# The order of work at the entry to a layer's experts, in a two-block transformer kernel on one core

## The chip, the core and the metric

The kernel runs on one core of a Trainium2 chip. The core has a matrix engine (TensorE, PE in the rows, with its weight loads as PEld), a vector engine (VectorE, DVE), a scalar engine (ScalarE, ACT), a general engine (GpSimd, POOL) and a queue engine (SyncE, SP) that here issues nearly all transfers from device memory. On-chip memory has 128 partitions; matrix products land in eight banks called ps0 to ps7. The metric is the device time of one execution in microseconds (us), and lower is better.

## What is computed

Two blocks over 256 tokens of width 1024, all in 32-bit floats. The first block has two layers; each is a mixer followed by a mixture of experts, and only the latter matters here. Cut to its core:

```python
def moe_ffn(u, w_router, b_router, w1, w3, w2, ws1, ws3, ws2):
    scores = jax.nn.sigmoid(xf @ w_router)                 # 256 tokens x 64 experts
    biased = scores + b_router                             # 4 of 8 groups, then 8 of 64 experts
    ...
    w = w / (jnp.sum(w, axis=-1, keepdims=True) + 1e-20) * ROUTED_SCALE
    ...                                                    # each expert gets the list of its tokens
    out = (silu(x @ w1[e]) * (x @ w3[e])) @ w2[e]          # 64 experts, inner width 256
    shared = (silu(xf @ ws1) * (xf @ ws3)) @ ws2           # one more expert, for every token
    return routed + shared
```

The second block (a gated recurrence and windowed attention) follows and is not touched.

## The kernel before

Each engine has a program of its own, written as a Python generator; the order in the code is the order on that engine. Engines wait for each other by named events: `K.pe("x")` marks an event, `te.wait_ge(*(yield ("x",)))` waits for it.

**Experts.** A layer's 64 experts are handled in 25 passes of 1, 2 or 4 experts (`PASS`). In a pass, `pe_up` multiplies the selected tokens `x_b` by w1 and then by w3, ACT and DVE form silu(w1 part) times w3 part, `pe_turn` turns it, `pe_down` multiplies by w2, and `pe_scatter` adds the result to the sums in banks 0 to 3 while the next pass already runs. `pe_selected(a)` picks the token rows of the passes 2a and 2a+1 by products with one-hot matrices that DVE makes (`dve_select`); the rows h are held as a high and a low part (`hx_hi`, `hx_lo`, tile `exact_rows`) so that the picking is exact. Experts 0 to 5 are fixed; the others are ordered by the length of their lists, so that SP must read an expert's number (`by_rank`) before it can load its weights. That number is made by `pe_lists_turned`, `pe_lists_ranked` and `dve_ranked`.

**Weights.** Each expert has three matrices of 1 MB, 192 MB per layer. A ring of 11 places of 1 MB, four places in `ar` and one in `cst` hold them: 16 MB in all. SP issues the loads in one fixed order, the order of use (`in_turn`), and each load first waits until the former holder of its place is used up. One load that waits holds up all behind it. `places()` deals out the places: the one that comes free first, by a table of nominal times, takes the next load. In pass numbers (a pass p uses w1 until p+0.2, w3 until p+0.45, w2 until p+1), the entry's own weights have the times of `RING_HELD`: router -6, shared w1 and w3 together -4, shared down (ws2) -2. By this table the loads at the start of a layer wait as follows: w1 of expert 4 for the router, w1 of 5 and w3 of 4 for the shared w1 and w3, w3 of 5 for shared down, w2 of 4 and 5 for w1 of experts 0 and 1, w1 of 8 and 9 for w3 of 0 and 1, w3 of 8 and 9 for w2 of 0 and 1, w2 of 8 and 9 for w1 of 2 and 3 (pass 1), w1 of 32 and 33 for w3 of 2 and 3, w1 of 34 and 35 for w2 of 2 and 3, that is for the end of pass 1's down products.

**The entry** (`pe_moe_start`, `act_moe_start`, `dve_moe_start`). After the norm, PE computes the router's logits by experts (64 x 256, L1909), ACT copies them out, PE turns them to tokens (L1921), ACT takes the sigmoid. DVE then chooses the experts (L2022 to L2057, event `chosen`) while PE does the shared products with ws1 and ws3 and turns h (L1930). Next PE counts the places in the lists, does two of the four shared down products (L1947), the token lists of the passes 0 and 1, `pe_selected(0)`, the turn of the lists, the other two shared down products and the ranking of the lists. Then pass 0 begins. On DVE, the products silu x w3 part (L2074) and the four subtractions that make `hx_lo` (L2081) come ahead of the places in the lists (L2085). `hx_lo` is written over h itself, so these subtractions wait until PE has turned all of h.

Of the kernel before, what the change touches and what calls it, by code (L numbers as in the profile page):

```python
# [412 lines left out]
def ring_plan(K):  # L413
# [24 lines left out]
    def shared(l):  # L438

        K.plan(("up", l, EXPERTS), 2, [(lambda f: f[:, 0:UNIT], I["ws1"][l].rearrange("(p k) f -> p (k f)", k=8)),  # L440
                                       (lambda f: f[:, UNIT:2 * UNIT], I["ws3"][l].rearrange("(p k) f -> p (k f)", k=8))])
        K.plan(("down", l, EXPERTS), 1, [(lambda f: k_major(f, D, 2), I["ws2"][l].rearrange("(j p) n -> p j n", j=2))])
# [1458 lines left out]
def pe_moe_start(K, l):  # L1901
    te, h = K.te, K.h
    yield from pe_norm(K, ("ffn", l), 256, K.sq8)
    w = k_major(K.flat["router", l], EXPERTS)
    rb = yield from K.bank(("logits", l), only=7)
    te.wait_ge(*(yield ("ring", "router", l)))
    for kk in range(8):
        te.wait_ge(*(yield ("h", ("ffn", l), kk, 0)))
        ins = te.matmul(rb[0:64, 0:256], w[:, kk, :], h[:, kk, :], start=(kk == 0), stop=(kk == 7))  # L1909
    ins.then_inc(*K.pe("logits_ps", l, ps=rb))  # L1910
    K.pe.also("used", "router", l)
    w = K.flat["up", l, EXPERTS][:, 0:2 * UNIT].rearrange("p (m k f) -> p m k f", m=2, k=8)
    te.wait_ge(*(yield ("ring", "up", l, EXPERTS)))
    for j, bank in enumerate((4, 5)):
        b = yield from K.bank(("shared_g", l, j), only=bank)
        products(te, b[:, 0:256], [(w[:, 0, kk, j * P:(j + 1) * P], h[:, kk, :]) for kk in range(8)])
        if j == 0:
            rb = yield from K.bank(("scores", l), only=6)
            te.wait_ge(*(yield ("logits", l)))
            for i in range(2):  # L1920
                ins = te.transpose(rb[:, i * 64:(i + 1) * 64], K.t_b[0:64, i * P:(i + 1) * P], K.ident[0:64, 0:64])  # L1921
            ins.then_inc(*K.pe("logits_turned", l, ps=rb))
        products(te, b[:, 256:512], [(w[:, 1, kk, j * P:(j + 1) * P], h[:, kk, :])
                                     for kk in range(8)]).then_inc(*K.pe("shared_up", l, j, ps=b))
    K.pe.also("used", "up", l, EXPERTS)
    for i in range(2):
        for q in range(2):
            b = yield from K.bank(("hx_lo", l, i, q), only=(6, 4, 5, 3)[2 * i + q])
            for k in range(4):
                ins = te.transpose(b[:, k * P:(k + 1) * P], h[:, 4 * q + k, i * P:(i + 1) * P], K.ident)  # L1930
            ins.then_inc(*K.pe("h_turned", l, i, q, ps=b))
# [8 lines left out]
    w2 = k_major(K.flat["down", l, EXPERTS], D, 2)  # L1940
    te.wait_ge(*(yield ("ring", "down", l, EXPERTS)))
    te.wait_ge(*(yield ("shared_g", l, 1)))
    for n in range(4):
# [5 lines left out]
        if n == 1:
            yield from pe_first_slots(K, l)  # L1950
            yield from pe_selected(K, l, 0)
            yield from pe_lists_turned(K, l)
    ins.then_inc(*K.pe("shared_down", l))
    K.pe.also("used", "down", l, EXPERTS)
    yield from pe_lists_ranked(K, l)
# [37 lines left out]
def act_moe_start(K, l):  # L1993
# [4 lines left out]
    ac.activation(K.t_b[0:64, :], K.ps["logits_ps", l][0:64, 0:256], ACT.Copy).then_inc(*K.act("logits", l))  # L1998
    ac.wait_ge(*(yield ("logits_turned", l)))
    ac.activation(K.sc, K.ps["logits_turned", l][:, 0:128].rearrange("p (i e) -> p i e", i=2),  # L2000
                  ACT.Sigmoid).then_inc(*K.act("scores", l))
# [3 lines left out]
    for i in range(2):  # L2005
        for q in range(2):
            ac.wait_ge(*(yield ("h_turned", l, i, q)))
            ac.activation(K.hx_hi_r[:, i, q * 512:(q + 1) * 512], K.ps["h_turned", l, i, q][:, :],
                          ACT.Copy).then_inc(*K.act("hx_hi", l, i, q))


def dve_moe_start(K, l):
# [59 lines left out]
    for j in range(2):  # L2072
        ve.wait_ge(*(yield ("shared_silu", l, j)))
        ve.tensor_tensor(K.gs[:, j, :], K.ss[:, j, :], K.ps["shared_up", l, j][:, 256:512],  # L2074
                         ALU.mult).then_inc(*K.dve("shared_g", l, j))
    ve.wait_ge(*(yield ("h_turned", l, 1, 1)))
    for i in range(2):
        for q in range(2):
            cols = slice(q * 512, (q + 1) * 512)
            ve.wait_ge(*(yield ("hx_hi", l, i, q)))  # L2080
            ve.tensor_tensor(K.hx_lo_r[:, i, cols], K.ps["h_turned", l, i, q][:, :], K.hx_hi[:, i, cols],  # L2081
                             ALU.subtract).then_inc(*K.dve("hx_lo", l, i, q))
# [1906 lines left out]
```

## Time and profile before

| | |
|---|---|
| three timed runs | 2398.68, 2399.28, 2400.83 us; median 2399.28 |
| the profiled execution, its own time | 2398.06 us |
| span in its trace | 2396.8 us |
| PE busy in the span | 2309.0 us, 96% |
| DVE, ACT, POOL busy | 814.2, 570.1, 135.6 us |
| moved by DMA | 673.21 MB, mean 281 GB/s |
| stretch of the expert passes, layer 0 and layer 1 | about 407 to 908 us and 1288 to 1790 us |

Busy time of PE is the time in which some product was in flight, so 96% does not say that the products set the pace in every stage. A transfer's time counts from its issue on SP, and a stage can be short of data while the mean rate is low.

### The profile page before, as it was taken

To read this page: it belongs to the slowest core of one execution; us is meant where nothing else is said; L and a number is where in the kernel's file an instruction comes from. 1 tells how busy PE (TensorE), PEld (TensorE's weight loads), DVE (VectorE), ACT (ScalarE), POOL (GpSimd) and SP (SyncE) were. 2 spreads that over 40 slices of the span, in tenths; PEclk is the share of its full clock that TensorE was granted. 3 is DMA by queue.
4 is the path that set the end of the run, shared out by engine and by line. 5 is a ranking of instruction groups with operands and counts; after the bars stand their busy time and mean duration, and the time that the engine had idled before them with its cause. 6 is when DMAs were issued, how large, how long until landed. Compare 5 with 4: busy or idle time off the path is not lost.

```text
span 2396.8 us, 34579 instructions
## 1 busy us (share of the span) xinstructions
PE 2309.0 (96%) x14027; PEld 1650.0 (69%) x14027; DVE 814.2 (34%) x2133; ACT 570.1 (24%) x1231; POOL 135.6 (6%) x179
## 2 busy tenths in 40 slices
PE   7999999999998998999999999998989999999998
PEld 4868897676665665768887676666657777854764
DVE  0376623212121111486524122211223544421264
ACT  2234412111111112224211111111113343321264
POOL 4040000000000000100000000000000000000110
PEclk9999999999999999999999999999999999999999
DMA  9785684999999996855776999999993543141110
GB/s 336 273 294 190 228 338 188 408 418 417 417 418 418 418 418 256 309 180 191 285 300 242 407 418 420 418 418 417 418 375 121 182 156 110 71 150 53 71 71 18
DMA packets 194619, 673.21 MB, mean 281 GB/s; under 512 B 14000, under 2 KB 50072, under 8 KB 144528
## 3 DMA queue, kind: packets, MB, share of 16 engines
q1 hardware_dynamic: 187776, 656.87, 70.5%
q0 software_dynamic: 6240, 13.99, 1.7%
q8 instruction: 115, 1.88, 0.3%
q14 instruction: 56, 0.46, 0.1%
q10 hardware_dynamic: 432, 0.01, 0.0%
HBM read 661.38 MB, written 9.45 MB: 280 GB/s over the span
## 4 chain that ended last, share of the span: by engine, by line
PE 88%; DMA 7%; DVE 1%; ACT 1%; issue 1%; SPq 1%; DVEq 0%; ACTq 0%
PE ps L282 49%; PE ps L2175 13%; PE ps L2212 7%; DMA ring<-in_w 7%; PE ps L2228 4%; PE ps L1757 3%; PE ps L1207 1%; PE ps L695 1%; PE ps L2924 1%; PE ps L3537 1%; DMA ring<-in_w_in 1%; PE ps L3702 1%; PE ps L3685 1%; PE ps L2198 1%; PE ps L3694 1%
## 5 line engine op out<-in xcount | busy, mean ns | idle before, releaser
L282 PE MATMUL ps<-hT,ring 128*128 128x256 f32 (+2 forms) x2352 | 541.1, 386 | 3.2 <-ACT ar L1577 1.9
L282 PEld LDWEIGHTS ps<-hT,ring 128*128 128x128 f32 (+1 forms) x2352 | 438.5, 189 | 99.7 <-issue 37.1
L2175 PE MATMUL ps<-ring,ar 128*32 128x256 f32 (+2 forms) x2688 | 314.3, 389 | 8.6 <-DMA ar<-in_w 4.7
L2175 PEld LDWEIGHTS ps<-ring,ar 128*32 128x32 f32 (+2 forms) x2688 | 189.1, 126 | 96.8 <-issue 20.4
L2175 PE MATMUL ps<-ar 128*64 128x256 f32 (+2 forms) x1120 | 179.5, 388 | 9.1 <-DMA ring<-in_w 9.1
L2212 PE MATMUL ps<-ring,ar 128*64 128x512 f32 (+2 forms) x728 | 159.7, 612 | 12.6 <-DMA ring<-in_w 7.3
L2495 DVE TENSOR_TENSOR ar<-ar,ps 128x256 f32<-128x256 f32 x50 | 21.1, 422 | 437.0 <-PE ps L2175 437.0
L2519 DVE SCALAR_TENSOR_TENSOR exact_parts<-ps,ar,exact_parts 128x512 fp32r<-128x512 f32 x100 | 75.1, 751 | 215.0 <-ACT exact_parts L2363 209.4
L282 PE MATMUL ps<-ring,ar 128*128 128x512 f32 x320 | 140.3, 595 | 0.0
L2363 ACT ACTIVATE exact_parts<-ps,ar 128x512 fp32r<-128x512 f32 x100 | 68.7, 687 | 291.0 <-PE ps L2212 272.8
L2175 PEld LDWEIGHTS ps<-ar 128*64 128x64 f32 (+2 forms) x1120 | 102.7, 129 | 46.2 <-issue 11.8
L2228 PE MATMUL ps<-exact_parts 128*128 128x512 f32 x400 | 108.1, 409 | 3.4 <-DVE exact_parts L2519 3.4
L282 PEld LDWEIGHTS ps<-ring,ar 128*128 128x128 f32 x320 | 60.7, 191 | 72.1 <-issue 70.8
L282 PE MATMUL ps<-xT,ring 128*128 128x256 f32 x480 | 107.9, 381 | 1.0 <-DVE ar L2476 1.0
L282 PE MATMUL ps<-exact_parts,exact_rows 128*128 128x256 f32 x832 | 107.1, 282 | 0.0
L282 PEld LDWEIGHTS ps<-exact_parts,exact_rows 128*128 128x128 f32 x832 | 101.2, 189 | 4.0 <-issue 2.5
L282 PEld LDWEIGHTS ps<-xT,ring 128*128 128x128 f32 x480 | 90.2, 190 | 15.7 <-issue 2.5
L282 PE MATMUL ps<-ring,hT 128*128 128x256 f32 (+1 forms) x384 | 100.0, 417 | 0.0
L2228 PEld LDWEIGHTS ps<-exact_parts 128*128 128x128 f32 x400 | 70.9, 188 | 41.3 <-issue 14.9
L282 PE MATMUL ps<-ar,ring 128*128 128x256 f32 (+1 forms) x416 | 98.8, 396 | 0.0
L2212 PEld LDWEIGHTS ps<-ring,ar 128*64 128x64 f32 (+2 forms) x728 | 45.3, 127 | 74.3 <-issue 68.2
L1353 DVE SCALAR_TENSOR_TENSOR ar<-ar,wdw 128x256 f32<-128x256 f32 x240 | 95.8, 478 | 0.0
(461 smaller groups left out, 2813.8 us busy)
## 6 DMA issues: line engine op xcount, KB each, us to landing
ring<-in_w SPq DMA_DIRECT2D x259, 1024.0 KB, 21.1
ar<-in_w SPq DMA_DIRECT2D x100, 1024.0 KB, 18.5
ring<-in_w_mod SPq DMA_DIRECT2D x36, 2048.0 KB, 11.9
ring<-in_w_in SPq DMA_DIRECT2D x28, 2048.0 KB, 12.0
ring<-in_ab_w_in SPq DMA_DIRECT2D x46, 1024.0 KB, 11.3
cst<-in_w SPq DMA_DIRECT2D x25, 1024.0 KB, 18.0
ring<-in_w_out SPq DMA_DIRECT2D x4, 2048.0 KB, 10.1
ar<-in_ab_w_in SPq DMA_DIRECT2D x8, 1024.0 KB, 24.5
```

What stands on the lines that cost most here:

```text
L282: ins = te.matmul(o, l, r, start=(first and i == 0), stop=(last and i == len(pairs) - 1), skip_group_check=lax)
L695: ins = te.matmul(b[32 * t:32 * t + 32, :], col(2 * t + s), w[:, 2 * t + s, :], start=(s == 0), stop=(s == 1))
L1207: ins = te.matmul(b[:, :], h[:, kk, i * P:(i + 1) * P], w[0][:, kk, :], start=(kk == 0), stop=(kk == 7))
L1353: ins = ve.scalar_tensor_tensor(K.acc[:, c, :], K.hpad[:, c, k:k + 256], tap, K.acc[:, c, :], ALU.mult, ALU.add)
L1757: ins = te.matmul(b[:, 0:256], w[kk // 4][:, kk % 4, k::8], K.merged[:, kk, :], start=(kk == 0), stop=(kk == 7))
L2175: ins = te.matmul(b[cols, 0:256], K.x_b[:, kk, in_pair(p, cols)], w[r][:, kk, :], start=(kk == 0), stop=(kk == 7))
L2198: ins = te.transpose(b[:, j * P:(j + 1) * P], K.g_b[:, j::2], K.ident)
L2212: ins = te.matmul(b[cols, :], K.t_b[:, j * P + cols.start:j * P + cols.stop], weights_down(K, l, r, j, q), start=(j == 0), stop=(j == 1))
L2228: ins = te.matmul(K.banks[2 * i + q][:, :], K.wT_r[:, p % 2, i * P:(i + 1) * P], part[:, q * 512:(q + 1) * 512], start=False, stop=False, ...
L2363: ac.activation(K.o_hi_r[:, q * 512:(q + 1) * 512], K.ps["down", l, p, q][:, :], ACT.Copy, scale=K.slot[:, p, 1:2]).then_inc(*K.act("o_hi" ...
L2519: ve.scalar_tensor_tensor(K.o_lo_r[:, cols], K.ps["down", l, p, q][:, :], K.slot[:, p, 1:2], K.o_hi_r[:, cols].bitcast(F32), ALU.mult, ALU ...
L2924: ins = te.matmul(b[:, cols], w[:, kk, c * P:(c + 1) * P], h[:, kk, cols], start=(kk == 0), stop=(kk == 7))
```

## The change

The change reorders the entry, and the pieces that move are these.

- The router's product is done by tokens: the weights loaded into the array are 128 columns of h and the moving side is the 64 columns of the router, once per half of the tokens, into banks 7 and 6. The copy on ACT and the two turns of the logits are gone; the sigmoid reads the banks in two pieces.
- Shared w1 and shared w3 become two loads and two items of the ring with times of their own (-4 and -2); shared down gets the time 0.75.
- On PE both ws1 products come right behind the router, then the places in the lists, the ws3 product of the first half, the token lists of the passes 0 and 1, the turn of the lists, the ws3 product of the second half, the turns of h, `pe_selected(0)` and at once pass 0.
- The ranking of the lists stands inside pass 0, between its w1 and w3 products; the four shared down products stand between pass 0's turn and its down products.
- On DVE the places in the lists, the selection of passes 0 and 1 and the ranking come ahead of the shared products and of the subtractions, which move to a new function `dve_rows` and go by halves of the width (q) first.
- The loads' waits change with the table: w1 of 5 waits for ws1, w3 of 4 for ws3, w3 of 5 and w2 of 4 for w1 of 0 and 1, w2 of 5 and w1 of 8 for w3 of 0 and 1, w1 of 9 for shared down. The waits of w3 of 8 up to w1 of 35 stay as they were. Later, places swap among loads that are used in the same part of a pass, apart from one: the load of the first half of ("mod2", 0, 2), ahead of layer 1, waits for w2 of the last pass instead of w3 and w1.

```diff
-NOTHING, THIRD, OUT, ROUTER, SHARED_UP, SHARED_DOWN = -12, -10, -8, -6, -4, -2
+NOTHING, THIRD, OUT, ROUTER, SHARED_W1, SHARED_W3, SHARED_DOWN = -12, -10, -8, -6, -4, -2, 0.75
...
@@ pe_moe_start
-    rb = yield from K.bank(("logits", l), only=7)
+    rb = []
+    for i in range(2):
+        rb.append((yield from K.bank(("scores", l, i), only=7 - i)))
     te.wait_ge(*(yield ("ring", "router", l)))
     for kk in range(8):
         te.wait_ge(*(yield ("h", ("ffn", l), kk, 0)))
-        ins = te.matmul(rb[0:64, 0:256], w[:, kk, :], h[:, kk, :], start=(kk == 0), stop=(kk == 7))
-    ins.then_inc(*K.pe("logits_ps", l, ps=rb))
+        for i in range(2):
+            ins = te.matmul(rb[i][:, 0:64], h[:, kk, i * P:(i + 1) * P], w[:, kk, :], start=(kk == 0), stop=(kk == 7))
+    ins.then_inc(*K.pe("logits_ps", l))
...
+    for j in range(2):
+        b = K.ps["shared", l, j] = yield from K.bank(("shared_g", l, j), only=2 + j)
+        pairs = [(w[:, kk, j * P:(j + 1) * P], h[:, kk, :]) for kk in range(8)]
+        ins = products(te, b[:, 0:256], pairs)
+    ins.then_inc(*K.pe("used", "ws1", l))
...
+    pe_shared_w3(K, l, 0, range(8))
+    yield from pe_first_slots(K, l)
+    yield from pe_lists_turned(K, l)
+    pe_shared_w3(K, l, 1, range(8))
+    for q in range(2):
+        for i in range(2):
+            b = yield from K.bank(("hx_lo", l, i, q), only=(6, 0, 1, 5)[2 * q + i])
+            for k in range(4):
+                ins = te.transpose(b[:, k * P:(k + 1) * P], h[:, 4 * q + k, i * P:(i + 1) * P], K.ident)
+            ins.then_inc(*K.pe("h_turned", l, i, q, ps=b))
+    yield from pe_selected(K, l, 0)
...
@@ pe_up
+        if name == "w1" and p == 0:
+            yield from pe_lists_ranked(K, l)
@@ pe_experts
         yield from pe_turn(K, l, p)
+        if p == 0:
+            yield from pe_shared_down(K, l)
@@ act_experts
-        if p > 0:
-            ac.wait_ge(*(yield ("g", l, p - 1)))
+        ac.wait_ge(*(yield (("g", l, p - 1) if p > 0 else ("ranked_ps", l))))
@@ new, called from dve_experts after dve_slots
+def dve_rows(K, l):
+    ve = K.ve
+    for j in range(2):
+        ve.wait_ge(*(yield ("shared_silu", l, j)))
+        ve.tensor_tensor(K.gs[:, j, :], K.ss[:, j, :], K.ps["shared_up", l, j][:, 256:512],
+                         ALU.mult).then_inc(*K.dve("shared_g", l, j))
+    ve.wait_ge(*(yield ("h_turned", l, 1, 1)))
+    for q in range(2):
+        for i in range(2):
+            cols = slice(q * 512, (q + 1) * 512)
+            ve.wait_ge(*(yield ("hx_hi", l, i, q)))
+            ve.tensor_tensor(K.hx_lo_r[:, i, cols], K.ps["h_turned", l, i, q][:, :], K.hx_hi[:, i, cols],
+                             ALU.subtract).then_inc(*K.dve("hx_lo", l, i, q))
```

On PE, at the head of the entry (L1909 the router, L1921 the turns of the logits, L282 with `hT,ring` the shared products, L1930 the turns of h), before:

```order
L1909 MATMUL ps<-hT,ring 64x256 x8
L282 MATMUL ps<-hT,ring 128x256 x8
L1921 MATMUL ps<-cst,ar 128x64 x2
L282 MATMUL ps<-hT,ring 128x256 x24
L1930 MATMUL ps<-cst,hT 128x128 x16
```

and now (L1912 is the router; L282 with `ar` and `cst` are the places in the lists):

```order
L1912 MATMUL ps<-ring,hT 128x64 x16
L282 MATMUL ps<-hT,ring 128x256 x16
L282 MATMUL ps<-ar 128x64
L282 MATMUL ps<-ar,cst 128x64
L282 MATMUL ps<-ar 128x64
```

The eight wide router products became sixteen narrow ones, the turns of the logits are gone, and the places stand behind 16 of the 32 shared products and ahead of the turns of h.

On PE, from the places to pass 0 (L1947 shared down, L2138 the token lists, L282 with `exact_rows` is `pe_selected(0)`, L1973 and L1975 the turn of the lists, L1989 the end of the ranking), before:

```order
L1947 MATMUL ps<-ring,ar 128x512 x4
L2138 MATMUL ps<-ar,exact_parts 64x2 x8
L282 MATMUL ps<-exact_parts,exact_rows 128x256 x32
L1973 MATMUL ps<-cst,ar 64x128 x2
L1975 MATMUL ps<-cst,ar 64x128 x2
L1947 MATMUL ps<-ring,ar 128x512 x4
L282 MATMUL ps<-ar,cst 128x64
L282 MATMUL ps<-ar 128x64
...
L1989 MATMUL ps<-ar 128x64 x4
L2175 MATMUL ps<-cst,ar 64x256
```

and now (L2141 the token lists, L1985 and L1987 the turn of the lists, L1940 the turns of h, L2178 the first of pass 0's w1 products):

```order
L282 MATMUL ps<-hT,ring 128x256 x8
L2141 MATMUL ps<-ar,exact_parts 64x2 x8
L1985 MATMUL ps<-cst,ar 64x128 x2
L1987 MATMUL ps<-cst,ar 64x128 x2
L282 MATMUL ps<-hT,ring 128x256 x8
L1940 MATMUL ps<-cst,hT 128x128 x16
L282 MATMUL ps<-exact_parts,exact_rows 128x256 x32
L2178 MATMUL ps<-cst,ar 64x256
```

Nothing stands any more between the turns of h and `pe_selected(0)`, nor between that and pass 0; the ranking and the eight shared down products went into the pass.

On DVE (L2074 the shared products of silu, L2081 the subtractions, L2085 to L2089 the places in the lists, L2376 the selection of passes 0 and 1), before:

```order
L2071 COPY ar<-ar 128x128
L2074 TENSOR_TENSOR ar<-ar,ps 128x256 x2
L2081 TENSOR_TENSOR exact_rows<-ps,exact_rows 128x512 x4
L2085 SCALAR_TENSOR_TENSOR ar<-ps,ar 128x128
L2088 TENSOR_SCALAR ar<-ar 128x128
L2089 COPY ar<-ps 64x1
L2376 TENSOR_SCALAR exact_parts<-cst,ar 128x64 x8
```

and now (L2088 to L2092 the places, L2379 the selection, L2478 the shared products, L2485 the subtractions, L2495 the copies of the selected rows):

```order
L2085 COPY ar<-ar 128x128
L2088 SCALAR_TENSOR_TENSOR ar<-ps,ar 128x128
L2091 TENSOR_SCALAR ar<-ar 128x128
L2092 COPY ar<-ps 64x1
L2379 TENSOR_SCALAR exact_parts<-cst,ar 128x64 x8
...
L2386 COPY ar<-ps 128x2 x2
L2478 TENSOR_TENSOR ar<-ar,ps 128x256 x2
L2485 TENSOR_TENSOR exact_rows<-ps,exact_rows 128x512 x4
L2495 COPY ar<-ps 128x512 x2
```

The subtractions now come last, directly ahead of the copies of the selected rows.

## Rows read from the trace of the kernel before

**Rows 1.** The page's chain that ended last, shares by engine.

```profile
PE 88%; DMA 7%; DVE 1%; ACT 1%; issue 1%; SPq 1%; DVEq 0%; ACTq 0%
```

**Rows 2.** That chain at the ends of both expert stretches: start, us, what.

```profile
875.85 26.64 DMA ring<-in_w
...
1754.08 30.33 DMA ring<-in_w
```

**Rows 3.** Stretches of the experts: length, busy by engine, clock, DMA share, GB/s.

```profile
437.00:438.00 1.00, 1.00 (x14) 0.64 (x12) 0.58 (x1) 0.38 (x1) 0.00 (x0) 1.00 1.11 295
438.00:439.00 1.00, 1.00 (x12) 0.70 (x10) 0.17 (x1) 0.00 (x0) 0.00 (x0) 1.00 0.50 164
438.60:902.50 463.90, 439.03 (x3580) 297.69 (x3576) 94.33 (x283) 59.97 (x102) 7.57 (x14) 0.99 1.02 417
...
1318.00:1320.00 2.00, 2.00 (x22) 1.34 (x20) 0.75 (x1) 0.02 (x1) 0.00 (x0) 1.00 0.91 270
...
1319.00:1784.50 465.50, 440.76 (x3583) 298.95 (x3578) 94.43 (x283) 59.97 (x102) 7.57 (x14) 0.99 1.01 415
```

**Rows 4.** SP's issues of loads in order of time: start, us, what.

```profile
411.30 0.33 SPq L579 DMA_DIRECT2D cst<-in_w  x1
...
436.84 1.44 SPq L579 DMA_DIRECT2D ring<-in_w  x2
```

**Rows 5.** PE in order of time, layer 0's entry: start, us, what, idle before.

```profile
370.92 5.32 PE L1909 MATMUL ps<-hT,ring 128*64 128x256 f32 x16 [2.23 <-ACT hT L1110]
376.18 3.72 PE L282 MATMUL ps<-hT,ring 128*128 128x256 f32 x16
379.83 0.34 PE L1921 MATMUL ps<-cst,ar 64*128 64x64 f32 x2
...
390.56 2.19 PE L1930 MATMUL ps<-cst,hT 128*128 128x128 f32 x16
392.58 0.33 PE L282 MATMUL ps<-ar 128*128 128x64 f32 x2
392.75 0.39 PE L282 MATMUL ps<-ar,cst 128*128 128x64 f32 x2
392.97 0.39 PE L282 MATMUL ps<-ar 128*128 128x64 f32 x2
...
394.06 3.70 PE L1947 MATMUL ps<-ring,ar 128*128 128x512 f32 x8
...
398.27 3.90 PE L282 MATMUL ps<-exact_parts,exact_rows 128*128 128x256 f32 x32
402.01 0.38 PE L1973 MATMUL ps<-cst,ar 128*64 128x128 f32 x2
...
407.57 0.43 PE L2175 MATMUL ps<-cst,ar 128*64 128x256 f32 x1
...
416.44 3.66 PE L2212 MATMUL ps<-ar 128*64 128x512 f32 x16 [0.61 <-DVE ar L2383]
419.90 7.11 PE L2175 MATMUL ps<-ring,ar 128*64 128x256 f32 x64
```

**Rows 6.** DVE in order of time, same place.

```profile
380.58 0.29 DVE L2022 TENSOR_TENSOR ar<-ar,par 128x128 f32<-128x128 f32 x1 [7.37 <-ACT ar L2000]
...
385.72 0.29 DVE L2057 TENSOR_TENSOR ar<-ar 128x128 f32<-128x128 f32 x1
...
392.78 2.48 DVE L2081 TENSOR_TENSOR exact_rows<-ps,exact_rows 128x512 fp32r<-128x512 f32 x4 [1.19 <-PE ps L1930]
...
402.21 0.69 DVE L2476 COPY ar<-ps 128x512 f32<-128x512 f32 x1 [1.12 <-PE ps L282]
```

**Rows 7.** Stretches of the router in layer 0 and layer 1, columns as in group 3.

```profile
370.94:374.35 3.41, 3.41 (x8) 1.82 (x9) 2.27 (x7) 2.63 (x7) 0.00 (x0) 0.50 1.01 428
...
1251.58:1254.99 3.41, 3.41 (x9) 1.81 (x10) 2.27 (x7) 2.62 (x7) 0.00 (x0) 0.50 1.01 428
```

**Rows 8.** Weight loads of 128 columns early in the run, half clock, then full: busy us, mean ns.

```profile
L1207 PEld LDWEIGHTS ps<-ring,hT 128*128 128x128 f32 x2 | 0.7, 337 | 1.0 <-ACT hT L1110 0.5 <-issue 0.5
...
L1207 PEld LDWEIGHTS ps<-ring,hT 128*128 128x128 f32 x21 | 4.0, 190 | 5.0 <-issue 5.0
```

More of the change, by code:

```diff
@@ L438, in shared @@
     def shared(l):
[L440 to L441 removed]
+        for n in ("ws1", "ws3"):
+            K.plan((n, l), 1, [(lambda f: f, I[n][l].rearrange("(p k) f -> p (k f)", k=8))])
         K.plan(("down", l, EXPERTS), 1, [(lambda f: k_major(f, D, 2), I["ws2"][l].rearrange("(j p) n -> p j n", j=2))])
@@ L1908, in pe_moe_start @@
         te.wait_ge(*(yield ("h", ("ffn", l), kk, 0)))
-        ins = te.matmul(rb[0:64, 0:256], w[:, kk, :], h[:, kk, :], start=(kk == 0), stop=(kk == 7))
-    ins.then_inc(*K.pe("logits_ps", l, ps=rb))
+        for i in range(2):
+            ins = te.matmul(rb[i][:, 0:64], h[:, kk, i * P:(i + 1) * P], w[:, kk, :], start=(kk == 0), stop=(kk == 7))
+    ins.then_inc(*K.pe("logits_ps", l))
     K.pe.also("used", "router", l)
[L1912 to L1925, printed above, removed]
-    for i in range(2):
[L1927 to L1931, printed above, removed]
+    for i in range(2):
+        K.ps["logits_ps", l, i] = rb[i]
+    w = k_major(K.flat["ws1", l], 256)
+    te.wait_ge(*(yield ("ring", "ws1", l)))
+    for j in range(2):
[3 more added lines that the diff above has]
+    ins.then_inc(*K.pe("used", "ws1", l))
+    te.wait_ge(*(yield ("ring", "ws3", l)))
     b = yield from K.bank(("places", l), ("counted", l), only=7)
@@ L1939, in pe_moe_start, with pe_shared_w3, pe_shared_down @@
                                     for i in range(2)]).then_inc(*K.pe("ranks", l, ps=b))
-    w2 = k_major(K.flat["down", l, EXPERTS], D, 2)
+    pe_shared_w3(K, l, 0, range(8))
[9 more added lines that the diff above has]
+    yield from pe_selected(K, l, 0)
+def pe_shared_w3(K, l, j, of):
+    w, b = k_major(K.flat["ws3", l], 256), K.ps["shared", l, j]
+    ins = products(K.te, b[:, 256:512], [(w[:, kk, j * P:(j + 1) * P], K.h[:, kk, :]) for kk in of],
+                   first=(0 in of), last=(7 in of))
+    if 7 in of:
+        ins.then_inc(*K.pe("shared_up", l, j, ps=b))
+    if j == 1:
+        K.pe.also("used", "ws3", l)
+def pe_shared_down(K, l):
+    te, w2 = K.te, k_major(K.flat["down", l, EXPERTS], D, 2)
     te.wait_ge(*(yield ("ring", "down", l, EXPERTS)))
@@ L1948, in pe_moe_start @@
                             stop=False, skip_group_check=True)
[L1949 to L1955, printed above, removed]
+    ins.then_inc(*K.pe("used", "down", l, EXPERTS))
 def pe_first_slots(K, l):
@@ L1997, in act_moe_start @@
     ac.wait_ge(*(yield ("logits_ps", l)))
[L1998 to L2001, printed above, removed]
+    for i in range(2):
+        ac.activation(K.sc[:, i, :], K.ps["logits_ps", l, i][:, 0:64], ACT.Sigmoid).then_inc(*K.act("scores", l, i))
     for j in range(2):
@@ L2004, in act_moe_start @@
         ac.activation(K.ss[:, j, :], K.ps["shared_up", l, j][:, 0:256], ACT.Silu).then_inc(*K.act("shared_silu", l, j))
-    for i in range(2):
-        for q in range(2):
+        if j == 0:
+            ac.wait_ge(*(yield ("lists_ps", l)))
+            ac.activation(K.turned_lists[0:64], K.ps["lists_ps", l][0:64, :].rearrange("p (a n) -> p a n", a=4),
+                          ACT.Copy).then_inc(*K.act("lists_turned", l))
+    for q in range(2):
+        for i in range(2):
             ac.wait_ge(*(yield ("h_turned", l, i, q)))
@@ L2071, in dve_moe_start @@
     ve.tensor_copy(K.tok_w[:, :, :, 1], mk).then_inc(*K.dve())
[L2072 to L2082, printed above, removed]
     ve.wait_ge(*(yield ("ranks", l)))
@@ L2484, in dve_experts @@
             yield from dve_slots(K, l, p)
+        yield from dve_rows(K, l)
         yield from selected(0)
```

11 lines of the change are left out of this document (5 added, 6 removed).

## The prediction

> **What bounds the kernel now.** The chain that ended last was read first. Its shares [rows 1] give PE 88% and DMA 7%, which reads like a kernel held by its products. The chain's pieces in order of time tell more: both expert stretches end on a transfer [rows 2]. The last weights of layer 0 were issued at 875.85 and landed 26.64 us later, at 902.49; in layer 1 it was 30.33 us from 1754.08. So the second view was the stretches [rows 3], and there the reader should compare the DMA share with PE's busy time. From 438.6 to 902.5, 463.9 us, the transfers ran at a share of 1.02 and 417 GB/s without a break, while PE was busy for 439.03 us: 24.9 us of it was spare. Layer 1 reads the same (465.5 us, 1.01, PE 440.76). The transfers set the end of both stretches, and PE waits for them on the way.
>
> A stream that never stops ends a fixed time after it last started. Where it last started is the question for this change. The single microseconds before that show it [rows 3]: 295 GB/s from 437 to 438 and 164 from 438 to 439. SP had issued the next two loads only at 436.84 [rows 4]; these are w1 of 34 and 35, which wait for the w2 places of pass 1. Layer 1 shows the like: 270 GB/s from 1318 to 1320 [rows 3]. All 16 MB were full or in use, and nothing was left to fetch until PE ended pass 1. So **the end of an expert stretch follows the time at which PE ends pass 1's down products**, us for us, and what the entry does earlier counts only as far as it moves that. The third view was therefore PE and DVE in order of time through the entry [rows 5, 6].
>
> PE has almost no hole there. From the router's first product at 370.92 to the end of pass 0's down products, at 419.90 where the next products start [rows 5], its only wait is the 0.61 us ahead of L2212, for a copy on DVE.
>
> **The change, part by part.** R is the time at which the router ends, 376.18 before.
>
> *Router.* Eight products of 256 columns become sixteen of 64; every 32-bit product shows as two rows, so 32 rows. At full clock two rows with 128 loaded columns and 64 moving ones take 0.22 us, from 392.75 to 392.97 [rows 5], so 0.11 each. In both layers the granted clock is at half, 1.2 GHz, for 3.41 us from the router's first product on, behind PE's wait of 2.23 us [rows 5, 7]. A weight load of 128 columns takes 337 ns at half and 190 ns at full clock [rows 8], so I take twice the pace, 0.22. Then 3.41 us hold 15.5 rows, the other 16.5 take 1.8 us, and R is 376.1: -0.1 us. The bounds: all 32 at 0.11 end at 374.4 (-1.8), all at 0.22 at 377.9 (+1.7).
>
> The Trainium skill, page "TensorE: Matmul & The Clock Gate", section "LDWEIGHTS (loading the stationary operand)", says that a weight load costs by its columns, P/1.2 ns, whatever the depth: 107 ns for 128 columns, which the trace's 0.11 us bears out at full clock. Its formula makes no difference between the clocks; by it alone the router would take 32 x 0.107 = 3.4 us and a layer would gain 1.8 us here. The two durations of the weight load differ with the clock, and I go by them.
>
> *Turns of the logits.* L1921 goes, with 0.3 us of PE [rows 5]. The copy on ACT goes too; neither it nor the sigmoid was on PE's path.
>
> *Choice and places.* Before, DVE began 0.41 us behind the end of L1921 at 380.17, which is one sigmoid with its hand-overs, and was done with `chosen` at 386.01, 5.43 us later [rows 5, 6]. Two sigmoid pieces cost at most twice that, so `chosen` comes by R+6.3. PE meanwhile does the ws1 products: 16 rows took 3.65 us [rows 5], so 32 take 7.3. The places don't wait; the margin is 1.0 us, and beyond it every us counts in full. The rest of DVE's list work then lies beside the ws3 products, two times 3.65 us, and is at no cost. The places, token lists, turn of the lists and ranking are the same products as before, in another place: nothing.
>
> *Subtractions.* Here a stall arises. Behind the turns of h PE now has `pe_selected(0)`, whose first half needs the first two pieces of `hx_lo`, and DVE starts these only when all of h is turned. Before, the turns ended at 392.58, DVE began at 392.78 and took 2.48 us for four [rows 5, 6]; PE had places, shared down and token lists to do until 398.27. Now it waits 0.2 + 2 x 0.6 = 1.4 us. The second half needs the other two 1.2 us later, while PE is busy for 1.87 us (half of 398.27 to 402.01), so that costs nothing. Bounds: 0.8, if one piece were in time, and 2.7, if PE waited for all four.
>
> *Copies of the selected rows.* w1 of pass 0 waits for all of `x_b`. The last copy on DVE began at 402.21, 0.2 us behind the products' end at 402.01, and took 0.69 [rows 5, 6]. Before, 5.5 us of other products lay over it; now nothing does: with the hand-over 0.95 us (0.7 to 1.1).
>
> *Ranking and shared down inside pass 0.* The ranking delays ACT's silu, but w3's products follow it on PE, so that is hidden. Shared down now stands where PE waited for the turned g, and its length covers the 0.61 us [rows 5]: -0.6.
>
> *Loads.* Shared down, two blocks of about 3.7 us, and the short ranking went into pass 0, and 0.6 us left it [rows 5]. With an end 1.35 us later it begins about 7 us earlier than 407.57, and w1's places come free 7 us earlier than 411.30 [rows 4]. But those transfers are the ones that filled the time up to 437 before; the next pair still waits for the end of pass 1. The load for w1 of 9 now waits for shared down, near 418; pass 3 uses it tens of us later. The swapped places later on are used up in the same parts of a pass. The one exception, a 2 MB load ahead of layer 1, goes out some 10 us later and needs about 5 us; the norm and the first projection of layer 1 stand before its use.
>
> Sum for one layer: 1.4 + 0.95 - 0.6 - 0.3 - 0.1 = **+1.35 us** at the end of pass 0, hence of pass 1 and of the stretch. Two layers: +2.7 us. The profiled execution took 2398.06 us, of which the span is 2396.8; with the change 2400.8. The median of the runs shown is 1.2 us above it, so they should give **2402.0 us**.
>
> **The rivals.**
>
> *The clock stays down (slower).* The new router loads weights for as long as it moves columns; the old one kept the array streaming. In the rows every rise to 2.4 GHz came after a stretch of dense products, and no row shows work like the new router's at half clock. If it does not lift the clock, all its rows run at half, R is 377.9, and the ws1 products run at half for as long as the old router did, 3.41 us [rows 7], before the clock rises: 1.8 + 1.7 = 3.5 us more in a layer. Then 2402.0 + 2 x 3.5 = **2409.0**. For it: that difference. Against it: PE is never idle in the new router, and another execution may not fall to half here at all, since 2.23 us is a short wait. It decides from the point where the clock is still at half 3.41 us after the first router product.
>
> The same page of the Trainium skill, section "Part 4: PE-mode transpose", says that transposes do not bring the full clock since they don't count as busy in the same way. No run here shows that; if the like holds for products bound by weight loads, this rival is what happens.
>
> *The earlier transfers win (faster).* Places come free up to 7 us earlier. If the stream did not run dry again before w1 of 34, each layer would gain up to those 7 us: 2399.3 - 14 = **2385**. For it: the long idle of the transfers ahead of 411 goes. Against it: ten loads of 1 MB lie between 411.3 and 437 and take 25 us at 417 GB/s, they end just as the pair at 436.84 is issued, and the last of them wait for w3 of pass 1, which does not come earlier. It decides by the GB/s around the end of pass 1.
>
> *The two stalls are longer.* All four subtractions on the path and 1.1 us for the copies: +2.8 a layer, **2404.9**.
>
> **How the numbers follow.** A measurement here can tell about 0.2%, 4.8 us, from no change. I give the forecast 0.57, with a range of its own from 2398.5 (the router at its lower bound) to 2404; the clock 0.30; the longer stalls 0.05; the earlier transfers 0.08. Forecast: same. Clock and longer stalls: slower, 0.35. Earlier transfers: faster, 0.08. For 8 in 10 the range runs from 2398.5 to the clock's case with half a us to spare, 2409.5.
>
> **What would show it.** In the new profile: waits of PE of about 1.4 us ahead of `pe_selected(0)`, for the subtractions, and of 0.95 us ahead of pass 0's w1, for the copies; no wait ahead of pass 0's down products; transfers that run dry again where pass 1 ends, at a time some 1.3 us later than 436.84; then no break to the end of the stretch. The clock rival shows as a granted clock of half beyond 374.4. The prediction is wrong if PE ends pass 1 earlier than before, if the transfers do not stop there, or if the stretch from there to the last landing is not the same length as before.

## The result and the profile after

The changed kernel takes 2406.4 us (median of 11 runs, 2402.95 to 2411.24) against 2399.0 (11 runs): a ratio of 1.0034, 95% interval 1.0026 to 1.0041. That is 6.2 to 9.8 us more, slower by a third of a per cent. The time lies inside the forecast range, but not with the case that was held likeliest (2402.0); it lies nearer to the rival in which the clock stays down (2409.0). The interval, 2405.2 to 2408.8 us, holds neither.

The profiled execution took 2410.87 us with a span of 2409.6. It is among the longest of the eleven, so its 12.8 us over the span of before is more than the median difference; where they lie is counted below.

The page's chain that ended last, shares by engine, of the changed kernel:

```profile
PE 87%; DMA 8%; DVE 2%; ACT 1%; issue 1%; SPq 1%; POOL 0%; DVEq 0%; ACTq 0%
```

and that chain in order of time (start, us, what), at the ends of both expert stretches:

```profile
879.23 27.45 DMA ar<-in_w
...
1764.63 31.00 DMA ring<-in_w
```

The shares say nothing new: the kernel is bound as before, and both stretches still end on a landing. The landings are what to read: 906.68 and 1795.63 us, against 902.49 and 1784.41 in [rows 2], so 4.2 and 11.2 us later.

The stretches of the changed kernel (length, busy by engine, granted clock, DMA share, GB/s), first both routers, then the ends of pass 1 and what follows them:

```profile
370.09:380.33 10.24, 10.15 (x40) 9.55 (x41) 4.84 (x28) 5.65 (x11) 0.00 (x0) 0.50 0.78 306
1257.56:1267.80 10.24, 10.24 (x39) 9.34 (x39) 5.27 (x32) 4.91 (x10) 0.00 (x0) 0.50 0.82 316
440.00:441.00 1.00, 1.00 (x10) 0.56 (x8) 0.72 (x2) 0.37 (x1) 0.00 (x0) 1.00 0.49 197
441.00:442.00 1.00, 1.00 (x14) 0.65 (x10) 0.65 (x1) 0.32 (x1) 0.00 (x0) 1.00 0.66 115
442.00:443.00 1.00, 1.00 (x12) 0.64 (x10) 0.10 (x1) 0.00 (x0) 0.00 (x0) 1.00 0.57 164
442.60:906.70 464.10, 439.37 (x3580) 298.80 (x3576) 94.34 (x283) 59.96 (x102) 7.57 (x14) 0.99 1.02 417
1328.00:1330.00 2.00, 2.00 (x22) 1.30 (x20) 0.75 (x1) 0.12 (x1) 0.00 (x0) 1.00 0.74 164
1329.50:1795.63 466.13, 442.75 (x3580) 299.14 (x3576) 94.43 (x283) 59.96 (x102) 7.57 (x14) 0.99 1.01 415
```

Two things stand here. The granted clock is at half for 10.24 us from the router on, in both layers, where [rows 7] had 3.41 us. And the transfers run dry at the end of pass 1 as before, about 4 us later than in [rows 3], and then run at 417 GB/s for 464.1 us: the stretch kept its length (463.9) and was only moved.

SP's first load for pass 0 in the changed kernel (start, us, what), 4 us earlier than in [rows 4]:

```profile
407.30 0.33 SPq L579 DMA_DIRECT2D cst<-in_w  x1
```

PE in order of time through layer 0's entry of the changed kernel (start, us, what, idle before):

```profile
370.18 7.06 PE L1912 MATMUL ps<-ring,hT 128*128 128x64 f32 x32 [2.23 <-ACT hT L1110]
377.04 8.75 PE L282 MATMUL ps<-hT,ring 128*128 128x256 f32 x32
385.63 0.33 PE L282 MATMUL ps<-ar 128*128 128x64 f32 x2
...
395.26 1.91 PE L1940 MATMUL ps<-cst,hT 128*128 128x128 f32 x16
398.64 4.00 PE L282 MATMUL ps<-exact_parts,exact_rows 128*128 128x256 f32 x32 [1.47 <-DVE exact_rows L2485]
403.59 0.40 PE L2178 MATMUL ps<-cst,ar 128*64 128x256 f32 x1 [0.94 <-issue]
...
413.08 0.50 PE L2203 MATMUL ps<-cst,ar 128*128 128x128 f32 x2
413.42 7.03 PE L1965 MATMUL ps<-ring,ar 128*128 128x512 f32 x16
420.38 3.66 PE L2217 MATMUL ps<-ar 128*64 128x512 f32 x16
423.87 0.38 PE L2178 MATMUL ps<-ring,ar 128*64 128x256 f32 x2
```

and at the head of layer 1's entry:

```profile
1256.91 6.47 PE L1912 MATMUL ps<-ring,hT 128*128 128x64 f32 x32 [2.23 <-ACT hT L1110]
1263.18 2.45 PE L282 MATMUL ps<-hT,ring 128*128 128x256 f32 x5
```

From the router's first product to the first product behind pass 0's down products is the measure for all that follows; call it the entry. It was 48.97 us, from 370.92 to 419.90 [rows 5], and is 53.69 now. The difference of 4.7 us can be read off line by line. The router takes 6.86 us to the next start, 1.6 more than 5.26. The 32 rows of ws1 take 8.59 where the same rows take 7.0 at full clock (in a run below), so 1.6 more. The two new idle times are 1.47 and 0.94. The 0.61 us ahead of the down products is gone, and so are 0.3 us for the turns of the logits. That makes 4.7.

DVE in order of time, the instruction that ends the choice (`chosen`) and then the two new idle times:

```profile
382.86 0.29 DVE L2071 TENSOR_TENSOR ar<-ar 128x128 f32<-128x128 f32 x1
...
397.21 2.48 DVE L2485 TENSOR_TENSOR exact_rows<-ps,exact_rows 128x512 fp32r<-128x512 f32 x4 [0.91 <-PE ps L1940]
...
402.69 0.69 DVE L2495 COPY ar<-ps 128x512 f32<-128x512 f32 x1 [1.19 <-PE ps L282]
```

The subtractions begin when all of h is turned, and PE starts 1.43 us behind their start, after two of the four. The last copy ends at 403.38, and w1's products begin 0.2 us later: the idle time that the view puts down to "issue" ends on a copy of DVE.

The 12.8 us of the profiled execution: -0.7 up to the first router, +4.7 and +4.8 for the entries (53.75 us in layer 1), +0.2 and +1.1 for what follows an entry up to the last landing, +1.2 between the landing of layer 0 and the router of layer 1, +1.6 behind the last landing. The small ones are no part of the change that could be named: in each of the ten traces the clock also falls at other places, and the median difference is smaller. The swapped load ahead of layer 1 shows no price: from the landing of layer 0 to the router of layer 1 the six kernels built on the changed one took 345.7 to 350.5 us, the four built on the kernel before 347.0 to 350.0.

### The profile page after: what moved, and what is told of

Same layout as the page of the kernel before. It is cut to its first block, busy times and chain, and to the rows that moved or that the text cites. A ratio compares the mean times of both kernels' runs of the same rounds, so it can differ in the third digit from the quotient of the medians.

```text
span 2409.6 us, 34633 instructions
## 1 busy us (share of the span) xinstructions
PE 2319.0 (96%) x14055; PEld 1660.2 (69%) x14055; DVE 814.4 (34%) x2133; ACT 569.2 (24%) x1231; POOL 135.7 (6%) x179
## 4 chain that ended last, share of the span: by engine, by line
PE 87%; DMA 8%; DVE 2%; ACT 1%; issue 1%; SPq 1%; POOL 0%; DVEq 0%; ACTq 0%
PE ps L282 49%; PE ps L2178 13%; PE ps L2217 7%; DMA ring<-in_w 6%; PE ps L2233 3%; PE ps L1757 3%; PE ps L1207 1%; PE ps L695 1%; PE ps L2944 1%; PE ps L3557 1%; DMA ar<-in_w 1%; DMA ring<-in_w_in 1%; PE ps L3705 1%; PE ps L2203 1%; SPq L579 1%
## 5 line engine op out<-in xcount | busy, mean ns | idle before, releaser
L282 PE MATMUL ps<-hT,ring 128*128 128x256 f32 (+2 forms) x2352 | 546.9, 388 | 3.2 <-ACT ar L1577 1.9
L282 PEld LDWEIGHTS ps<-hT,ring 128*128 128x128 f32 (+1 forms) x2352 | 442.5, 191 | 100.3 <-issue 36.4
L2178 PE MATMUL ps<-ring,ar 128*64 128x256 f32 (+2 forms) x2704 | 336.0, 390 | 10.6 <-DMA ar<-in_w 6.3
L2178 PEld LDWEIGHTS ps<-ring,ar 128*64 128x64 f32 (+2 forms) x2704 | 200.8, 127 | 99.6 <-issue 22.4
L2178 PE MATMUL ps<-ar 128*64 128x256 f32 (+2 forms) x1072 | 206.5, 389 | 7.1 <-DMA ring<-in_w 7.1
L2217 PE MATMUL ps<-ring,ar 128*32 128x512 f32 (+1 forms) x704 | 170.2, 616 | 13.5 <-DVE ar L2386 6.1
L2178 PEld LDWEIGHTS ps<-ar 128*64 128x64 f32 (+2 forms) x1072 | 113.9, 129 | 46.7 <-issue 15.7
L282 PE MATMUL ps<-ring,ar 128*128 128x512 f32 x320 | 139.8, 593 | 0.9 <-DVE ar L3786 0.9
L282 PE MATMUL ps<-exact_parts,exact_rows 128*128 128x256 f32 x832 | 107.8, 283 | 2.9 <-DVE exact_rows L2485 2.9
L282 PEld LDWEIGHTS ps<-ring,ar 128*128 128x128 f32 x320 | 60.3, 190 | 72.8 <-issue 70.7
L282 PE MATMUL ps<-xT,ring 128*128 128x256 f32 x480 | 108.7, 381 | 1.0 <-DVE ar L2495 1.0
L282 PEld LDWEIGHTS ps<-exact_parts,exact_rows 128*128 128x128 f32 x832 | 101.9, 189 | 7.3 <-DVE exact_rows L2485 3.4
L2217 PE MATMUL ps<-ar 128*32 128x512 f32 (+2 forms) x280 | 104.4, 632 | 1.2 <-DVE ar L2386 1.2
L282 PEld LDWEIGHTS ps<-xT,ring 128*128 128x128 f32 x480 | 90.4, 190 | 15.3 <-issue 2.1
L282 PE MATMUL ps<-ring,hT 128*128 128x256 f32 (+1 forms) x384 | 100.0, 417 | 0.0
L282 PE MATMUL ps<-ar,ring 128*128 128x256 f32 (+1 forms) x416 | 98.8, 396 | 0.0
L2217 PEld LDWEIGHTS ps<-ring,ar 128*32 128x32 f32 (+1 forms) x704 | 47.8, 127 | 70.7 <-issue 67.1
## 6 DMA issues: line engine op xcount, KB each, us to landing
ring<-in_ab_w_in SPq DMA_DIRECT2D x46, 1024.0 KB, 11.2
```

The source lines that it names most:

```text
L282: ins = te.matmul(o, l, r, start=(first and i == 0), stop=(last and i == len(pairs) - 1), skip_group_check=lax)
L2178: ins = te.matmul(b[cols, 0:256], K.x_b[:, kk, in_pair(p, cols)], w[r][:, kk, :], start=(kk == 0), stop=(kk == 7))
L2217: ins = te.matmul(b[cols, :], K.t_b[:, j * P + cols.start:j * P + cols.stop], weights_down(K, l, r, j, q), start=(j == 0), stop=(j == 1))
```

## The experiments

All ratios are to the kernel before, run on the same chip (2398.1 us for the new router alone, the old router, the clock held in the changed kernel and the waits covered; 2398.31 for the other four).

**The new router alone.** The kernel before with the new router's products, its two sigmoids, and no turn of the logits:

```diff
-        ins = te.matmul(rb[0:64, 0:256], w[:, kk, :], h[:, kk, :], start=(kk == 0), stop=(kk == 7))
+        for i in range(2):
+            ins = te.matmul(rb[i][:, 0:64], h[:, kk, i * P:(i + 1) * P], w[:, kk, :], start=(kk == 0), stop=(kk == 7))
...
-            te.wait_ge(*(yield ("logits", l)))
-            for i in range(2):
-                ins = te.transpose(rb[:, i * 64:(i + 1) * 64], K.t_b[0:64, i * P:(i + 1) * P], K.ident[0:64, 0:64])
```

> The kernel before with the new router alone: 32 rows of 64 columns, no copy and no turn of the logits. Theory (the clock stays down through such a router): the granted clock is at half for about 10 us from the router's first product instead of 3.41; router +1.6 us, shared products behind it +1.5, turns -0.3, so +2.8 us in a layer and 2404.6 us, about two thirds of the whole slowdown. Rival (the slowdown is the two new stalls and the moved loads; the router itself costs nothing): the turns alone are gone, 2398.4 us, at half clock for 3.41 us as before.

Measured: 2402.95 us, ratio 1.0023 (1.0014 to 1.0033), which is 3.4 to 7.9 us more. The router alone makes the kernel slower. Its profiled execution shows both cases, since the clock fell in layer 1 and not in layer 0 (stretches of that kernel, columns as above):

```profile
366.98:370.58 3.60, 3.60 (x33) 3.60 (x33) 2.29 (x7) 3.58 (x8) 0.00 (x0) 1.00 1.03 435
1247.30:1257.54 10.24, 10.24 (x40) 9.43 (x40) 5.12 (x31) 5.11 (x10) 0.00 (x0) 0.50 0.84 323
```

In layer 0 the same 32 rows took 3.60 us at full clock and the entry 46.82 us; in layer 1 the clock was at half for 10.24 us and the entry took 51.77. One program, one execution, and 4.95 us between its two layers.

**The old router in the changed kernel.** Its logits are copied and turned at once:

```diff
-        for i in range(2):
-            ins = te.matmul(rb[i][:, 0:64], h[:, kk, i * P:(i + 1) * P], w[:, kk, :], start=(kk == 0), stop=(kk == 7))
+        ins = te.matmul(rb[0:64, 0:256], w[:, kk, :], h[:, kk, :], start=(kk == 0), stop=(kk == 7))
...
+    rb = yield from K.bank(("scores", l), only=6)
+    te.wait_ge(*(yield ("logits", l)))
+    for i in range(2):
+        ins = te.transpose(rb[:, i * 64:(i + 1) * 64], K.t_b[0:64, i * P:(i + 1) * P], K.ident[0:64, 0:64])
```

> The changed kernel with the old router, eight products of 256 columns, whose logits are copied and turned at once behind it. Theory (clock): half clock for 3.41 us only, which takes 3.1 us off a layer, while PE waits about 0.7 us for the copy and turns for 0.3, so -2.1 a layer and 2402.2 us. Rival (the stalls and the moved loads): nothing is taken off and the turn adds 1.0 a layer, 2408.4 us.

Measured: 2404.53 us, ratio 1.0024 (1.0014 to 1.0035), 3.4 to 8.4 us more than before. By the time alone this doesn't decide: it lies between the two expectations, and its interval overlaps that of the changed kernel. The trace does (a stretch, then PE in order of time):

```profile
370.74:374.16 3.42, 3.42 (x9) 1.82 (x10) 2.23 (x7) 2.60 (x7) 0.00 (x0) 0.50 1.01 426
374.16:377.57 3.41, 2.94 (x15) 1.87 (x14) 0.00 (x0) 1.50 (x2) 0.00 (x0) 1.00 0.99 332
```

```profile
370.69 5.32 PE L1909 MATMUL ps<-hT,ring 128*64 128x256 f32 x16 [2.23 <-ACT hT L1110]
376.48 0.33 PE L1915 MATMUL ps<-cst,ar 64*128 64x64 f32 x2 [0.47 <-ACT ar L2010]
376.74 1.56 PE L282 MATMUL ps<-hT,ring 128*128 128x256 f32 x6
```

With the old router the clock is back after 3.4 us, and the entries take 51.18 and 51.25 us: 2.5 less than the changed kernel, 2.2 more than before.

**The clock held through the wait.** Four products on constants, read by nothing, in PE's idle time ahead of the router; the same in the changed kernel and in the kernel before:

```diff
+    pe_keep_busy(K, rb[0], 4)
     te.wait_ge(*(yield ("ring", "router", l)))
```

In the changed kernel:

> The changed kernel with four products of 256 columns on constants, whose result nothing reads, in PE's wait of some 2.3 us ahead of the router. Theory (clock): it does not fall there, the router's 32 rows take 3.5 us in place of 7.06 and ws1's products 7.1 in place of 8.59, so -4.9 us a layer and 2396.6 us; the places don't wait, since the choice ends 6.1 us behind the router and ws1 takes 7.1. Rival (the clock is no part of the slowdown, or the end of the stretch doesn't follow PE): 2406.4 us.

In the kernel before:

> The kernel before with the same four products on constants in PE's wait ahead of its router. Theory (what the clock costs is read from the router): the old router loses only the one stretch of 3.41 us at half clock, so its layer gains 1.6 us and the whole 3.2: 2394.9 us against 2398.1 for the kernel before in the last runs. The changed kernel gained 8.2 us from the same products. Rival (the products bring something else than the clock, the same for both kernels): 2390 us.

Measured: 2398.16 us in the changed kernel, ratio 1.0000 (0.9991 to 1.0009), and 2396.66 in the kernel before, ratio 0.9995 (0.9986 to 1.0004). The same four products take the changed kernel from 1.0034 to no difference, and do little for the kernel before. Both gained less than expected, 8.2 of 9.8 us and 1.2 to 1.7 of 3.2; a likely reason stands under the table. PE in order of time, the changed kernel with them:

```profile
367.49 1.89 PE L681 MATMUL ps<-cst 128*128 128x256 f32 x8
369.89 3.76 PE L1913 MATMUL ps<-ring,hT 128*128 128x64 f32 x32 [0.51 <-ACT hT L1110]
373.48 7.13 PE L282 MATMUL ps<-hT,ring 128*128 128x256 f32 x32
380.44 0.33 PE L282 MATMUL ps<-ar 128*128 128x64 f32 x2
```

and the kernel before with them:

```profile
368.30 3.64 PE L1910 MATMUL ps<-hT,ring 128*64 128x256 f32 x16 [0.51 <-ACT hT L1110]
371.86 3.72 PE L282 MATMUL ps<-hT,ring 128*128 128x256 f32 x16
```

The stretch behind the router's start in each, first the changed kernel:

```profile
369.89:380.13 10.24, 10.24 (x63) 9.46 (x64) 7.65 (x43) 5.55 (x11) 0.00 (x0) 1.00 0.85 341
368.30:371.71 3.41, 3.41 (x16) 2.06 (x16) 2.28 (x7) 2.64 (x7) 0.00 (x0) 1.00 1.03 435
```

With the clock at full the two routers take the same time, 3.59 and 3.56 us. The entries are 48.66 and 48.71 us in the changed kernel, 47.42 and 47.43 in the kernel before: 1.25 us apart.

**The two waits covered.** Shared down is split over them:

```diff
+    yield from pe_shared_down(K, l, (2, 3))
     yield from pe_selected(K, l, 0)
+    yield from pe_shared_down(K, l, (0,))
...
         if p == 0:
-            yield from pe_shared_down(K, l)
+            yield from pe_shared_down(K, l, (1,))
```

> The changed kernel with shared down split: its third and fourth quarter stand behind the turns of h, over the subtractions, its first behind the products that select pass 0's rows, over the copies, its second stays in pass 0. Theory (the end of a stretch follows PE's entry us for us): the stalls of 1.47 and 0.94 us go, -2.4 us a layer, 2401.6 us; the clock's part, some 6 us, stays. Rival (the transfers set the end whatever PE's entry does): no change, 2406.4 us.

Measured: 2402.43 us, ratio 1.0016 (1.0007 to 1.0025). Against the changed kernel's 1.0034 that is 4 us less, near the 4.8 expected. PE in order of time shows both idle times gone:

```profile
395.45 3.60 PE L1967 MATMUL ps<-ring,ar 128*128 128x512 f32 x8
398.48 4.22 PE L282 MATMUL ps<-exact_parts,exact_rows 128*128 128x256 f32 x32
402.54 1.88 PE L1967 MATMUL ps<-ring,ar 128*128 128x512 f32 x4
```

Its entries are 50.92 and 51.04 us, 2.7 less, and the clock is still at half for 10.24 us in both layers.

**Wide moving columns.** The changed kernel's router, order and weight loads as they are, but each row moves its 64 columns four times (the copies are read by nothing):

```diff
-            ins = te.matmul(rb[i][:, 0:64], h[:, kk, i * P:(i + 1) * P], w[:, kk, :], start=(kk == 0), stop=(kk == 7))
+            ins = te.matmul(rb[i][:, 0:256].rearrange("p (a e) -> p a e", a=4), h[:, kk, i * P:(i + 1) * P],
+                            w[:, kk, :].unsqueeze(1).to_broadcast([P, 4, 64]), start=(kk == 0), stop=(kk == 7))
```

> The changed kernel whose router moves each 64 weight columns four times: the same 32 rows and the same weight loads of 128 columns, but 256 moving columns a row as in the old router. One look, for the clock. Theory (it is the narrow moving side that does not lift the clock): where the clock falls to half at the router, it is back at full 3.41 us later, as with the old router; the 32 rows take about 3.41 + 24 x 0.22 = 8.7 us, the ws1 products behind them 7.1. Rival (it is the weight loads, or the order by tokens): half for 10.24 us, the 32 rows at some 0.43 each.

Measured: one run, 2403.75 us, of which the trace is what counts. In layer 0 the clock did not fall. In layer 1 it did (stretches, then PE in order of time):

```profile
1250.39:1253.81 3.42, 3.42 (x9) 2.68 (x9) 1.40 (x5) 3.04 (x6) 0.00 (x0) 0.50 1.00 419
1253.81:1257.22 3.41, 3.41 (x17) 2.98 (x16) 0.00 (x0) 0.00 (x0) 0.00 (x0) 1.00 0.47 192
```

```profile
1249.49 8.83 PE L1912 MATMUL ps<-ring,hT 128*128 128x256 f32 x32 [2.23 <-ACT hT L1110]
1258.16 7.07 PE L282 MATMUL ps<-hT,ring 128*128 128x256 f32 x32
```

The clock was back after 3.4 us, in the middle of the router, where the narrow rows were at half for 10.24 us in all five of their falls. The order by tokens and the loads of 128 columns are the same in both, so neither of them explains the longer stretch; what differs is the moving side. This rests on one fall in one execution. The rows took 8.67 us to the next start, as expected.

**Delay put in by hand.** Sixteen products on constants ahead of the ranking, in the kernel before:

```diff
     b = yield from K.bank(("ranked_kept", l))
+    pe_keep_busy(K, b, 16)
```

> The kernel before with sixteen more products of 256 columns on constants ahead of the ranking, before pass 0: some 6.9 us of PE's time a layer that changes nothing else. Theory (the end of an expert stretch follows PE's entry us for us): pass 1 ends 6.9 us later and so does the last landing, +13.8 us, 2411.9 us. Rival (the transfers set the end, PE has slack): 2398 to 2401 us.

Measured: 2411.86 us, ratio 1.0057 (1.0044 to 1.0071), 13.5 us over the median of before: us for us. Layer 1's entry, where the clock fell as before, took 55.89, which is 6.92 more. The added products in layer 0, and the landings that end both stretches:

```profile
403.76 7.07 PE L681 MATMUL ps<-cst 128*128 128x256 f32 x32
```

```profile
880.08 26.86 DMA ring<-in_w
...
1765.17 31.09 DMA ring<-in_w
```

The landings stand at 906.94 and 1796.26 us, 482.3 and 484.3 behind the entries' ends, as before (482.6 and 483.9).

**Both remedies.** The changed kernel with the four products and the split:

> The changed kernel with the four products ahead of the router and the split shared down together. From the router's first product to the end of pass 0's down products it should take 48.66 - 2.77 = 45.9 us a layer, against 48.98 in the kernel before. Theory (us for us in this direction too): -3.1 us a layer, 2391.9 us, faster than both kernels. Rival (below the length of before, the transfers that fill the time up to the end of pass 1 become the bound): 2396 to 2398 us.

Measured: 2394.68 us, ratio 0.9987 (0.9977 to 0.9996): faster than both kernels, by 1.0 to 5.5 us against the one before. Its entries are 45.97 and 46.02 us as expected, but the time stands between the 2391.9 expected and the rival's 2396. Some of that is the reference: the expectation took a fall at every router of the kernel before as certain (under the table); the rest lies inside the interval. The trace speaks against the rival so far: the last landings come 482.8 and 484.6 us behind the entries' ends, as in the other kernels. But at the end of pass 1 (stretches of that kernel) the transfers hardly stop any more:

```profile
428.00:432.00 4.00, 4.00 (x30) 1.99 (x28) 3.00 (x13) 1.38 (x2) 0.00 (x0) 1.00 0.99 410
431.00:432.00 1.00, 1.00 (x12) 0.69 (x10) 0.63 (x1) 0.00 (x0) 0.00 (x0) 1.00 0.93 369
432.00:433.00 1.00, 1.00 (x14) 0.64 (x12) 0.00 (x0) 0.00 (x0) 0.00 (x0) 1.00 0.82 320
```

The lowest single microseconds read 369 and 320 GB/s, against 295 and 164 in [rows 3]. So a still shorter entry may have little more to give; no run tried one.

All ten traces together: the entry in both layers, how long the clock was at half at the router, and the time from the entry's end to the last landing of the stretch (us):

| kernel | entry, layers 0 and 1 | at half | to the last landing | ratio |
|---|---|---|---|---|
| before | 48.97, 48.97 | 3.41, 3.41 | 482.6, 483.9 | 1 |
| changed | 53.69, 53.75 | 10.24, 10.24 | 482.8, 485.0 | 1.0034 |
| new router alone | 46.82, 51.77 | 0, 10.24 | 483.0, 484.8 | 1.0023 |
| old router in the changed | 51.18, 51.25 | 3.41, 3.41 | 483.1, 484.6 | 1.0024 |
| clock held, changed | 48.66, 48.71 | 0, 0 | 482.4, 484.4 | 1.0000 |
| clock held, before | 47.42, 47.43 | 0, 0 | 482.6, 484.5 | 0.9995 |
| waits covered | 50.92, 51.04 | 10.24, 10.24 | 482.9, 485.8 | 1.0016 |
| both remedies | 45.97, 46.02 | 0, 0 | 482.8, 484.6 | 0.9987 |
| wide columns | 52.01, 53.82 | 0, 3.41 | 482.7, 484.3 | one run |
| delay by hand | 54.33, 55.89 | 0, 3.41 | 482.3, 484.3 | 1.0057 |

The column before the last is the law that the prediction rested on: over ten kernels and 10 us of entry it moves by under 1 us in layer 0 and 2 us in layer 1. The column "at half" says the rest: without the four products the clock fell at 11 of 14 routers, behind the same idle time of PE (2.23 to 2.24 us); with them at none of six. Whether it falls differs from one execution to the next, and from layer to layer. A fall costs the old router's entry 1.55 us (48.97 - 47.42) and the new one's 5.0 (53.69 - 48.66). So with falls in all entries the changed kernel would be slower by 4.7 + 4.8 = 9.5 us, with none by 2 x 1.25 = 2.5, and with 11 of 14 by 8.0 (an estimate from those shares). The measured 6.2 to 9.8 fit; the shares come from one execution of each kernel. By the same count the expectations for the clock held were too good, since they took the fall as certain in the kernel that they started from (it gives 7.9 us in place of 9.8 and 2.4 in place of 3.2); for both remedies it gives 5.3 us in place of 6.2, inside the measured 1.0 to 5.5.

## Why the prediction was right and wrong

**The time lies in the range, but not by the sum.** The sum gave 2402.0; the range up to 2409.5 had been drawn to the clock's case, and that is what put the measured time inside it. By the prediction's own measure of noise, 4.8 us, the kernel is slower by 6.2 to 9.8 us, a case to which it gave 0.35 against 0.57 for no change.

**The law was right.** Experts' stretches end a fixed time behind PE's entry, in both directions, for delays put in by hand and for gains. The rival in which earlier transfers win has fallen: the loads of pass 0 go out earlier, at 407.30 in place of 411.30 [rows 4], and the transfers run dry again at the end of pass 1, for longer than before.

**The waits were right in size.** The subtractions were forecast at 1.4 us and took 1.47, the copies 0.95 and 0.94; the wait of 0.61 us went, and the turns of the logits with 0.3. Those four terms make +1.5 us. The longer stalls (rival) did not come. With the clock held in both kernels the entries differ by 1.25 us where the forecast said 1.35.

**The choice was right.** `chosen` came at 383.15, 6.1 us behind the router's end (forecast 6.3), and the places did not wait. The margin was 2.5 us and not 1.0, only because ws1's products were slow: with the clock held the same event came 0.7 us ahead of the places (379.71 and 380.44).

**The router's term failed.** It stood at -0.1 us. The sentence "Then 3.41 us hold 15.5 rows, the other 16.5 take 1.8 us" let the clock rise at the time at which it had risen under the old router, though the work below it was other work. Measured in layer 0: +1.6 for the router, all of whose 32 rows ran at 0.21 us, the doubled pace, and +1.6 for ws1 behind it. That is 3.2 us a layer, the clock rival's 3.5 nearly, and two thirds of the slowdown. The prediction had named what spoke for it, that every rise had come behind dense products; it gave it 0.30, though no row showed the clock rise behind work like the new router's.

The Trainium skill, page "TensorE: Matmul & The Clock Gate", section "LDWEIGHTS (loading the stationary operand)", has the weight load cost by its columns, 107 ns for 128, which would make the router 3.4 us (an estimate from that figure). The trace agrees at full clock (3.59 us for 32 rows) and not at half (6.86); and even at full clock nothing is gained by it, since the old router takes 3.56 there. The same page of the Trainium skill, section "Part 4: PE-mode transpose", says that transposes don't count as busy in the way that products do. No run here shows that of transposes; what the runs show is the router's 32 rows of 64 moving columns at half clock for 6.86 us, with PE busy throughout.

## What to carry to other kernels

A product that is cut into narrow pieces has to be priced at both clocks, and the work behind it too, if an idle time stands ahead of it: look in the trace at what PE did before each rise of the granted clock, and don't let other work raise it in a sum. Where PE waits ahead of such work, a few products that nothing reads may be worth more than the reordering; and a wait that a reordering uncovers is best covered by moving independent products into it, in pieces of the length of the wait. What an entry is worth is read at the place where the transfers run dry; where they no longer do, no run here shows that a shorter entry gains anything.

## What the runs showed of the hardware

The granted clock stayed at half while the profile showed PE busy without a break: 10.15 of 10.24 us in layer 0 and 10.24 of 10.24 in layer 1, of which the first 6.9 us (layer 0) and 5.6 us (layer 1) were the router's rows of 64 moving columns. It rose 3.3 us (layer 0) and 4.6 us (layer 1) after the products of 256 columns had begun. With the same loads and 256 moving columns the clock was back at full after 3.4 us. So the busy column alone did not tell here whether the clock would rise.

The same idle time of 2.23 us brought the clock down at 11 of 14 routers; in three executions it did so in layer 1 and not in layer 0. Such falls are not the main part of the spread between runs of one kernel, since the changed kernel spreads by 7.8 us with the clock held at the router (2394.67 to 2402.46) and by 8.3 without.
